# A kernel of two transformer stages with expert look-up: fourteen more load buffers for the first up units, spreading from unit 64, and five row slots

## The chip, the cores and the metric

The kernel runs on one core of one Trainium2 chip. Its time is the device time of one execution in microseconds; the median of several runs is compared. Engines are named as in the profile: PE is TensorE, DVE the vector engine, ACT the scalar engine, POOL the pool engine (GpSimd), SP the queue engine that issues loads.

## What is computed

A block with attention and a state-space mixer is followed by a second block, whose last part is the place of the change: for 256 tokens h a look-up in 16,384 experts. A query picks 16 experts for each of eight heads, u and v are tables of 16,384 rows of 1,024 numbers, and

```python
def chunk(ht):
    t = ht.shape[0]
    q = (ht @ wq).reshape(t, PEER_HEADS, 2, PEER_DK)
    sa = jnp.einsum('thd,hnd->thn', q[:, :, 0], keys[0]).astype(jnp.float32)
    sb = jnp.einsum('thd,hnd->thn', q[:, :, 1], keys[1]).astype(jnp.float32)
    ...
    eidx = jnp.take_along_axis(cidx, pos, axis=-1)
    g = jax.nn.softmax(top, axis=-1).astype(ht.dtype)
    u = u_tab[eidx]
    v = v_tab[eidx]
    a = jax.nn.gelu(jnp.einsum('thkd,td->thk', u, ht))
    return jnp.einsum('thk,thkd->td', g * a, v)
```

## The kernel before, in words

The tokens of the look-up are treated in two ways. For the first ND = 176 tokens the kernel multiplies with the whole tables: 128 "up units" of u and 128 "down units" of v, each 128 experts wide and 512 KB, are loaded one after the other. For the other 80 tokens it gathers the picked rows: 80 "row passes" with rows of u and 80 with rows of v, each pass one indirect load of 128 rows of 4 KB and one DVE instruction over 128x1024.

In order of time the last part has these stages. The query projection (16 units `peer_wq`). The early up units 0 to N_EARLY - 1 = 49 on PE, while DVE picks the experts (`pick`), first for the second half of the tokens, whose row numbers are known early, then for the first. ACT writes the gelu of two units at once into X (`u_early`). Then the late up units 50 to 127. Beside them the gates are spread: for each of ND/4 = 44 steps s (four tokens each) DVE, POOL and ACT write one-hot rows of the picked experts (`one_hot`), PE multiplies them into a bank ("spread", four small matmuls), and DVE and ACT multiply the bank into X (`empty_gates`, `copy_rest`). Late units are multiplied with their gates by `u_late`. At last the down stage: each of 256 chunks (two per down unit) is cut into a high part by ACT and a low part by DVE, and PE multiplies it with X.

Row passes run on DVE in the order of the list `passes`: N_FIRST = 16 inside the second pick, then those up to N_BETWEEN = 23 before the spread steps, those up to N_LATE = 94 within them, and the remaining 66 within the down stage, evenly over 250 chunk steps (`pass_step`).

What sets the order is written out by hand. The generator `spread_steps` yields, for every half unit, which one-hot, spread, emptying and row pass stand there, and PE, DVE, ACT and POOL each run through the same sequence and pick their own; every engine carries out its instructions in that order and waits for semaphores. One-hot s needs the buffer of spread s - 2. Gather n (`gather`, on POOL) needs the slot of pass n - 4.

Loads of weights are issued by SP in the order of `plan`, into a ring of NRAW = 4 buffers: up unit n + 4 is loaded when unit n is done, a down unit when the one four before it has been cut. In the trace of the kernel before, L609 is SP's load, L615 PE's matmul, L2093 a row pass of u, L1342 a row pass of v, L3125 a gather, L3136 a one-hot on POOL, L1336 and L1339 DVE's tensor_tensor and tensor_scalar (one-hots among them), L2232 and L2229 ACT's copies and activations.

## Time and profile before

| what | us |
|---|---|
| median of 3 runs | 1458.18 |
| lowest, highest | 1457.92, 1467.05 |
| the profiled execution | 1462.89 |
| its span, first to last instruction | 1461.1 |
| PE busy | 1400.8 (96%) |
| DVE busy | 1143.9 (78%) |
| POOL busy | 392.2 (27%) |
| DMA, mean over the span | 249 GB/s |

A windows row gives, for a stretch, each engine's busy time with the number of its instructions, then the granted share of PE's clock, the busy share of the 16 DMA engines and what they moved. A timeline row gives start, duration, instruction, and in brackets the idle time before it with what ended it. In the profile a matmul of two fp32 operands stands as two records; the count of an up unit is so 16. Times in rows count from the start of the span.

### The profile page before, as it was taken

The numbers are of one execution on the slowest core, as the hardware profiler recorded it, in microseconds if no ns is written. First come the engines' busy times: TensorE is split into PE (matmuls) and PEld (weight loads), VectorE is DVE, ScalarE is ACT, GpSimd is POOL, SyncE is SP. The second block draws the span as 40 slices with busy tenths as digits, with TensorE's granted clock in tenths as the row PEclk, the third lists the DMA queues.
The fourth block names the chain that finished last, engine by engine and source line by source line (L and its number), as shares of the span: only waits on it lengthen the run. The fifth ranks groups of instructions, "written<-read, shape, count | busy, mean of one in ns | idle before, by whom it ended". The sixth has DMA issues, their size and how long they took to land.

```text
span 1461.1 us, 28173 instructions
## 1 busy us (share of the span) xinstructions
PE 1400.8 (96%) x10866; PEld 1301.5 (89%) x10866; DVE 1143.9 (78%) x2296; ACT 773.2 (53%) x1576; POOL 392.2 (27%) x421
## 2 busy tenths in 40 slices
PE   7999999998999999999889999999999999999998
PEld 6668998877879988888789999899999999999998
DVE  4676996787668889866657899676777699899987
ACT  5785886753355555566454200344443466666655
POOL 7620001000300000001100022589887343333430
PEclk9999999999999999999999999999999999999999
DMA  7305554651369899652344699989999899999995
GB/s 241 101 30 169 179 170 151 192 180 40 138 219 345 310 323 344 244 172 88 111 127 143 186 334 334 373 313 363 356 351 363 310 363 352 359 353 349 358 340 177
DMA packets 100003, 363.47 MB, mean 249 GB/s; under 512 B 11152, under 2 KB 11152, under 8 KB 99744
## 3 DMA queue, kind: packets, MB, share of 16 engines
q1 hardware_dynamic: 67536, 244.45, 48.5%
q0 software_dynamic: 24560, 89.95, 17.0%
q10 hardware_dynamic: 7776, 27.27, 5.1%
q8 instruction: 89, 1.46, 0.4%
q14 instruction: 42, 0.34, 0.1%
HBM read 360.58 MB, written 1.05 MB: 248 GB/s over the span
## 4 chain that ended last, share of the span: by engine, by line
PE 74%; DVE 9%; DMA 9%; ACT 4%; issue 3%; POOL 0%; DVEq 0%; ACTq 0%; SPq 0%
PE ps L615 72%; DMA arena<-in_peer_v 5%; DVE w_lo L1336 3%; DVE arena L1336 2%; ACT w_hi L2232 2%; DVE arena L1342 2%; ACT arena L2229 1%; DMA arena<-in_u_rows,arena 1%; DMA arena<-in_peer_u 1%; PE ps L821 1%; DMA arena<-in_w_ff 1%; PE ps L948 0%; DVE act_hi_lo L1336 0%; PE ps L778 0%; DVE arena L2093 0%
## 5 line engine op out<-in xcount | busy, mean ns | idle before, releaser
L1336 DVE TENSOR_TENSOR w_lo<-arena,w_hi 128x512 fp32r<-128x512 f32 x680 | 455.4, 689 | 166.5 <-ACT w_hi L2232 162.3
L2232 ACT ACTIVATE w_hi<-arena 128x512 fp32r<-128x512 f32 x680 | 417.6, 625 | 294.3 <-PE ps L615 219.8
L615 PE MATMUL ps<-act_hi_lo,w_hi 128*128 128x256 f32 (+1 forms) x2496 | 554.8, 315 | 12.4 <-DVE w_lo L1336 5.2
L615 PE MATMUL ps<-arena 128*128 128x176 f32 (+9 forms) x4858 | 480.7, 280 | 23.5 <-DVE arena L1339 7.5
L615 PEld LDWEIGHTS ps<-arena 128*128 128x128 f32 (+3 forms) x4858 | 455.2, 166 | 44.9 <-issue 17.4
L615 PE MATMUL ps<-act_hi_lo,w_lo 128*128 128x176 f32 (+1 forms) x1760 | 455.7, 259 | 0.1
L615 PEld LDWEIGHTS ps<-act_hi_lo,w_hi 128*128 128x128 f32 x2496 | 421.6, 190 | 21.3 <-ACT w_hi L2232 9.1
L615 PEld LDWEIGHTS ps<-act_hi_lo,w_lo 128*128 128x128 f32 x1760 | 336.4, 191 | 0.1
L615 PE MATMUL ps<-w_hi,act_hi_lo 128*128 128x512 f32 (+2 forms) x960 | 304.5, 392 | 11.5 <-DVE w_lo L1336 5.0
L1336 DVE TENSOR_TENSOR arena<-arena 128x512 f32<-128x512 f32 (+17 forms) x298 | 183.7, 625 | 63.2 <-ACT arena L2229 56.9
L615 PEld LDWEIGHTS ps<-w_hi,act_hi_lo 128*128 128x128 f32 x960 | 181.0, 190 | 55.3 <-issue 13.7
L615 PE MATMUL ps<-w_lo,act_hi_lo 128*128 128x512 f32 (+2 forms) x480 | 185.9, 387 | 0.0
L3125 POOL DMA_INDIRECT arena<-in_v_rows,arena x80 | 123.7, 1546 | 192.4 <-DVE arena L1342 179.9
L2229 ACT ACTIVATE arena<-ps 128x512 f32<-128x512 f32 (+19 forms) x138 | 55.3, 429 | 188.8 <-PE ps L615 172.5
L3125 POOL DMA_INDIRECT arena<-in_u_rows,arena x80 | 95.0, 1187 | 204.3 <-DVE arena L1946 128.9
L2229 ACT ACTIVATE arena<-arena 128x128 f32<-128x128 f32 (+8 forms) x256 | 122.2, 491 | 49.2 <-DVE arena L1336 19.6
L2961 POOL TENSOR_TENSOR arena<-arena 128x32 f32<-128x32 f32 (+1 forms) x130 | 55.5, 441 | 317.1 <-ACT arena L2232 271.2
L2232 ACT ACTIVATE arena<-ps 128x512 f32<-128x512 f32 (+21 forms) x160 | 70.2, 454 | 108.4 <-DVE arena L1336 71.8
L2093 DVE SCALAR_TENSOR_TENSOR arena<-arena 128x1024 f32<-128x1024 f32 x80 | 97.6, 1228 | 17.3 <-DMA arena<-in_u_rows,arena 15.9
L1342 DVE SCALAR_TENSOR_TENSOR arena<-arena 128x1024 f32<-128x1024 f32 (+5 forms) x100 | 107.1, 1071 | 1.5 <-DMA arena<-in_v_rows,arena 0.9
L615 PEld LDWEIGHTS ps<-w_lo,act_hi_lo 128*128 128x128 f32 x480 | 91.2, 190 | 16.6
L3136 POOL TENSOR_SCALAR arena<-arena 128x128 f32<-128x128 f32 x66 | 88.9, 1350 | 4.9 <-DVE arena L2021 1.5
(105 smaller groups left out, 681.3 us busy)
## 6 DMA issues: line engine op xcount, KB each, us to landing
arena<-in_w_ff SPq DMA_DIRECT2D x128, 512.0 KB
arena<-in_peer_u SPq DMA_DIRECT2D x128, 512.0 KB
arena<-in_peer_v SPq DMA_DIRECT2D x128, 512.0 KB
arena<-in_w_ada ACTq DMA_DIRECT2D x48, 512.0 KB, 5.5
arena<-in_w_glu SPq DMA_DIRECT2D x16, 512.0 KB
arena<-in_peer_wq SPq DMA_DIRECT2D x16, 512.0 KB
arena<-in_w_in SPq DMA_DIRECT2D x12, 512.0 KB
arena<-in_w_conv SPq DMA_DIRECT2D x12, 512.0 KB
```

The source lines that it names most:

```text
L615: return e.matmul(o, l, r, start=start, stop=stop)
L821: ins = e.transpose(pb(bk, 2 * nk, 128)[:, h * nk + kb, :], att.s(u)[:, h, kb * 128:(kb + 1) * 128], ident)
L1336: return e.tensor_tensor(o, a, b, op)
L1342: return e.scalar_tensor_tensor(out=o, in0=a, scalar=s, in1=b, op0=op0, op1=op1)
L2093: ins = e.scalar_tensor_tensor(out=slot, in0=slot, scalar=1.0, in1=row_h[g], op0=ALU.mult, op1=ALU.mult, accum_out=a)
L2229: return e.activation(o, a, f, **k)
L2232: return e.activation(o, a, ACT.Copy)
L2961: return e.tensor_tensor(o, a, b, op)
L3125: e.indirect_dma_start(row_slot(n), None, T[f"{kind}_rows"], bass.IndirectOffsetOnAxis(ap=row_at[:, p:p + 1].bitcast(U32), axis=0)).then_i ...
L3136: ins = e.tensor_scalar(ob[:, k, :], iota, ibT[:, n:n + 1], gT[:, n:n + 1], ALU.is_equal, ALU.mult)
```

## The change

Fourteen buffers join the ring for the up units: ten in the place of the mixed activations (the low end of the arena, where X will be written), four at 16384. They serve units up to the one whose result is written there (`last_u`), the last of them up to unit 63. Up units 0 to 11 are loaded among the query loads: eight after query load 3, one each after 5, 7, 9 and 11 (`U_AHEAD`). From unit 12 on a load goes into the buffer that has been in use longest of those that may still serve it. N_EARLY goes from 50 to 64, N_BETWEEN from 23 to 36 (20 passes between the second pick and the spread steps, where there were 7), N_LATE from 94 to 104. Row slots go from four to five, so that gather n needs the slot of pass n - 5. The gelu of the first 32 rows' products is done ahead of the spread steps, and the copy of the tokens to hU is used from unit N_EARLY + 2.

```diff
--- before.py
+++ after.py
@@
 EPS = 1e-6
 UNIT = 1024
 NRAW = 4
+N_LOW, N_MORE = 10, 14
+U_AHEAD = {3: range(8), 5: (8,), 7: (9,), 9: (10,), 11: (11,)}
 CUT = 512
 NHL = 4
+N_SLOTS = 5
 AHEAD = 3
-N_EARLY = 50
+N_EARLY = 64
 ND = 176
 
 OFF_X = 0
...
@@
     len_of = {name: sum(plan[i][0] == name for i, _ in chunks) for name in end}
     first_u = next(i for i, x in enumerate(plan) if x[0] == "peer_u")
 
+    buffers = [ar[:, OFF_RING + UNIT * n:OFF_RING + UNIT * n + UNIT] for n in range(NRAW)]
+    buffers += [ar[:, UNIT * n:UNIT * n + UNIT] for n in range(N_LOW)]
+    buffers += [ar[:, 16384 + UNIT * n:16384 + UNIT * n + UNIT] for n in range(4)]
+    free_after = ["ring"] * NRAW + ["mixed"] * N_LOW + ["window"] * 2 + ["keys"] * 2
+    last_u = [127] * NRAW + [min(N_EARLY - 1, 2 * (UNIT * n // (2 * ND)) + 1) for n in range(N_LOW)]
+    last_u += [N_EARLY - 1] * 4
+    first_order = list(range(NRAW, NRAW + N_LOW + 2)) + [None] * NRAW + list(range(NRAW + N_LOW + 2, NRAW + N_MORE))
+
+    buffer_of, used_before, load_of = [], [], []
+    used = {}
+    for i in range(len(plan)):
+        u = i - first_u
+        b = i % NRAW
+        if 0 <= u < len(first_order):
+            b = b if first_order[u] is None else first_order[u]
+        elif 0 <= u < 128:
+            b = min((x for x in used if last_u[x] >= u), key=lambda x: used[x][0])
+        buffer_of.append(b)
+        used_before.append(used[b][0] if b in used else None)
+        load_of.append(used[b][1] + 1 if b in used else 1)
+        used[b] = i, load_of[i]
+
     def raw(i):
-        o = OFF_RING + (i % NRAW) * UNIT
-        return ar[:, o:o + plan[i][2]]
+        return buffers[buffer_of[i]][:, 0:plan[i][2]]
 
     def raw_in(i):
-        return ring_in[i % NRAW], 16 * (i // NRAW + 1)
+        return ring_in[buffer_of[i]], 16 * load_of[i]
+
+    def load_order():
+        first_q = first_u - 16
+        early = [u for us in U_AHEAD.values() for u in us]
+        for i in range(len(plan)):
+            if i - first_u not in early:
+                yield i
+            for u in U_AHEAD.get(i - first_q, ()):
+                yield first_u + u
 
     def raw_piece(n):
         i, c = chunks[n]
@@
 
     passes = [("u", p) for p in range(N_ROWS)] + [("v", p) for p in range(N_ROWS)]
     nth = {x: n for n, x in enumerate(passes)}
-    N_PASS, N_FIRST, N_BETWEEN, N_LATE, N_ONES = len(passes), 16, 23, 94, 3
-    U_COPY = N_EARLY + 4
+    N_PASS, N_FIRST, N_BETWEEN, N_LATE, N_ONES = len(passes), 16, 36, 104, 3
+    U_COPY = N_EARLY + 2
 
     def row_group(p):
         return sum(p >= f for f in ROW_FIRST[1:3])
@@
     row_bank = (6, 7, 2, 3, 4, 5)
 
     def row_slot(g):
-        return V(QP + 1024 * (g % 4), 1024)
+        return V((QP, QP + 1024, QP + 2048, QP + 3072, OFF_GB + 1024)[g % N_SLOTS], 1024)
 
     def pass_step(n):
 
@@
     def sync_program(e):
         e.dma_start(V(OFF_SM, SMN), T["small"]).then_inc(small_in, 16)
         e.wait_ge(x_in[0], 16)
-        for i, (_, source, _, _) in enumerate(plan):
-            before = i - NRAW
+        for i in load_order():
+            source, before, free = plan[i][1], used_before[i], free_after[buffer_of[i]]
             if i == 1:
                 e.wait_ge(x_in[1], 16)
-            if before >= 0 and plan[before][0] == "peer_u":
+            if before is not None and plan[before][0] == "peer_u":
                 e.wait_ge(*u_done["unit", before - first_u])
-            elif before >= 0:
+            elif before is not None:
                 e.wait_ge(lo_cut.sem, last_cut[before] + 1)
-            e.dma_start(raw(i), source).then_inc(ring_in[i % NRAW], 16)
+            elif free == "mixed":
+                for c in (0, 2, 4, 6):
+                    e.wait_ge(*alo_cut["mixed1", c])
+            elif free == "window":
+                e.wait_ge(*masked["window", window_att.n - 1])
+            elif free == "keys":
+                e.wait_ge(*mm_done["key_scores", 0, 3])
+            e.dma_start(raw(i), source).then_inc(ring_in[buffer_of[i]], 16)
 
     def tensor_program(e):
         at = dict(n=0)
@@
                 e.wait_ge(*bent["rows", g])
                 tt(products, products, row_g[:, own], ALU.mult).then_inc(*rows_v("gated", g))
                 e.wait_ge(*rows_v["gated", g])
-            e.wait_ge(gather_in[n % 4], 16 * (n // 4 + 1))
+            e.wait_ge(gather_in[n % N_SLOTS], 16 * (n // N_SLOTS + 1))
             if kind == "u":
                 ins = e.scalar_tensor_tensor(out=slot, in0=slot, scalar=1.0, in1=row_h[g], op0=ALU.mult,
                                              op1=ALU.mult, accum_out=a)
@@
                 e.wait_ge(*gated["spread", ND // 4 - 1])
             elif j == 1:
                 e.wait_ge(*gated["u", 63])
+        for n in sorted(after_products):
+            if n < N_BETWEEN:
+                row_gelu(after_products[n])
         for what, *a in spread_steps():
             if what == "units":
                 copy_rest(waiting)
@@
         def gather(n):
 
             kind, p = passes[n]
-            if n >= 4:
-                e.wait_ge(*rows_v["pass", n - 4])
+            if n >= N_SLOTS:
+                e.wait_ge(*rows_v["pass", n - N_SLOTS])
             e.indirect_dma_start(row_slot(n), None, T[f"{kind}_rows"],
                                  bass.IndirectOffsetOnAxis(ap=row_at[:, p:p + 1].bitcast(U32), axis=0)
-                                 ).then_inc(gather_in[n % 4], 16)
+                                 ).then_inc(gather_in[n % N_SLOTS], 16)
 
         def one_hot(s):
             oa, ob = one_hots(s)
@@
             ins.then_inc(*ones_p("b", s))
 
         e.wait_ge(*pick_v["rows"])
-        for n in range(N_FIRST + 4):
+        for n in range(N_FIRST + N_SLOTS):
             gather(n)
         e.wait_ge(*bank[6]["picked", 0])
         one_hot(0)
-        for n in range(N_FIRST + 4, N_BETWEEN + 3):
-            if n == N_FIRST + 6:
+        for n in range(N_FIRST + N_SLOTS, N_BETWEEN + N_SLOTS - 1):
+            if n == N_FIRST + N_SLOTS + 2:
                 one_hot(1)
-            if n == N_BETWEEN + 2:
+            if n == N_BETWEEN + N_SLOTS - 2:
                 one_hot(2)
             gather(n)
         for what, *a in spread_steps():
             if what == "ones" and a[0] >= N_ONES:
                 one_hot(*a)
             elif what == "row":
-                gather(a[0] + 3)
-        for n in range(N_LATE + 3, N_PASS):
+                gather(a[0] + N_SLOTS - 1)
+        for n in range(N_LATE + N_SLOTS - 1, N_PASS):
             gather(n)
 
     programs = ((nc.tensor, tensor_program), (nc.vector, vector_program), (nc.scalar, scalar_program),
```

On SP the query and up loads now alternate (in the rows, `in_peer_wq` is the query projection's weights and `in_peer_u` the up units'). SP's place around the query projection, before:

```order
L609 DMA arena<-in_w_conv 128x1024 x12
L609 DMA arena<-in_w_out 128x1024 x8
L609 DMA arena<-in_peer_wq 128x1024 x16
L609 DMA arena<-in_peer_u 128x1024 x128
L609 DMA arena<-in_peer_v 128x1024 x128
```

and now:

```order
L649 DMA arena<-in_w_out 128x1024 x8
L649 DMA arena<-in_peer_wq 128x1024 x4
L649 DMA arena<-in_peer_u 128x1024 x8
L649 DMA arena<-in_peer_wq 128x1024 x2
L649 DMA arena<-in_peer_u 128x1024
L649 DMA arena<-in_peer_wq 128x1024 x2
L649 DMA arena<-in_peer_u 128x1024
L649 DMA arena<-in_peer_wq 128x1024 x2
L649 DMA arena<-in_peer_u 128x1024
L649 DMA arena<-in_peer_wq 128x1024 x2
```

Twelve up loads stand ahead of the last query loads, the other 116 behind them.

On POOL, from the first gather on (`in_u_rows` is a gather, L3136 and L3179 are one-hots, one for even steps and two for odd ones), before:

```order
L3125 DMA arena<-in_u_rows,arena 128x1024 x20
L3136 TENSOR_SCALAR arena<-arena 128x128
L3125 DMA arena<-in_u_rows,arena 128x1024 x2
L3136 TENSOR_SCALAR arena<-arena 128x128 x2
L3125 DMA arena<-in_u_rows,arena 128x1024 x3
L3136 TENSOR_SCALAR arena<-arena 128x128
L3125 DMA arena<-in_u_rows,arena 128x1024 x6
L3136 TENSOR_SCALAR arena<-arena 128x128 x2
L3125 DMA arena<-in_u_rows,arena 128x1024
L3136 TENSOR_SCALAR arena<-arena 128x128
L3125 DMA arena<-in_u_rows,arena 128x1024 x2
L3136 TENSOR_SCALAR arena<-arena 128x128 x2
```

and now:

```order
L3168 DMA arena<-in_u_rows,arena 128x1024 x21
L3179 TENSOR_SCALAR arena<-arena 128x128
L3168 DMA arena<-in_u_rows,arena 128x1024 x2
L3179 TENSOR_SCALAR arena<-arena 128x128 x2
L3168 DMA arena<-in_u_rows,arena 128x1024 x16
L3179 TENSOR_SCALAR arena<-arena 128x128
L3168 DMA arena<-in_u_rows,arena 128x1024 x5
L3179 TENSOR_SCALAR arena<-arena 128x128 x2
L3168 DMA arena<-in_u_rows,arena 128x1024 x2
L3179 TENSOR_SCALAR arena<-arena 128x128
L3168 DMA arena<-in_u_rows,arena 128x1024
L3179 TENSOR_SCALAR arena<-arena 128x128 x2
```

Sixteen gathers instead of three stand between one-hots 1 and 2, five instead of six between one-hots 2 and 3; after that the pattern of one or two gathers to a one-hot step goes on.

On DVE, from the seventeenth row pass on (L2093 and L2133; the pair L1336 and L1339, L1376 and L1379 over 128x512 and 128x128 is a one-hot, the form `ps,arena` an emptying), before:

```order
L2093 SCALAR_TENSOR_TENSOR arena<-arena 128x1024 x6
L1336 TENSOR_TENSOR arena<-arena 128x512
L1339 TENSOR_SCALAR arena<-arena 128x128
L2093 SCALAR_TENSOR_TENSOR arena<-arena 128x1024 x4
L1336 TENSOR_TENSOR arena<-ps,arena 128x54x4
L2093 SCALAR_TENSOR_TENSOR arena<-arena 128x1024
L1336 TENSOR_TENSOR arena<-arena 128x2x4
L2093 SCALAR_TENSOR_TENSOR arena<-arena 128x1024
L1336 TENSOR_TENSOR arena<-arena 128x512
L1339 TENSOR_SCALAR arena<-arena 128x128
```

and now:

```order
L2133 SCALAR_TENSOR_TENSOR arena<-arena 128x1024 x19
L1376 TENSOR_TENSOR arena<-arena 128x512
L1379 TENSOR_SCALAR arena<-arena 128x128
L2133 SCALAR_TENSOR_TENSOR arena<-arena 128x1024 x3
L1376 TENSOR_TENSOR arena<-ps,arena 128x66x4
L2133 SCALAR_TENSOR_TENSOR arena<-arena 128x1024
L1376 TENSOR_TENSOR arena<-arena 128x2x4
L2133 SCALAR_TENSOR_TENSOR arena<-arena 128x1024
L1376 TENSOR_TENSOR arena<-arena 128x512
L1379 TENSOR_SCALAR arena<-arena 128x128
```

Nineteen passes instead of six stand ahead of one-hot 2, and five instead of six between one-hots 2 and 3.

## Rows read from the trace of the kernel before

**Rows 1.** The page: busy time, share of the span, instructions of each engine.

```profile
PE 1400.8 (96%) x10866; PEld 1301.5 (89%) x10866; DVE 1143.9 (78%) x2296; ACT 773.2 (53%) x1576; POOL 392.2 (27%) x421
```

**Rows 2.** Busy time by stage; the first row names the columns.

```profile
core 0: us, PE busy (x) PEld busy (x) DVE busy (x) ACT busy (x) POOL busy (x), PEclk, DMA share, GB/s
716.00:797.00 81.00, 75.49 (x558) 70.72 (x558) 52.53 (x164) 39.90 (x76) 1.12 (x2) 1.00 0.43 133
...
847.00:921.00 74.00, 72.77 (x486) 71.93 (x485) 72.47 (x253) 9.84 (x18) 23.25 (x21) 1.00 0.95 349
...
953.00:1145.00 192.00, 191.78 (x1357) 191.81 (x1358) 141.93 (x270) 76.85 (x226) 162.38 (x128) 0.99 0.96 352
...
1158.00:1440.00 282.00, 275.26 (x2005) 271.51 (x2005) 257.37 (x377) 174.41 (x310) 100.72 (x62) 1.00 0.95 347
```

**Rows 3.** Busy time by ten microseconds, same columns.

```profile
940.00:950.00 10.00, 6.69 (x46) 6.18 (x44) 5.67 (x11) 1.62 (x5) 5.24 (x5) 0.98 1.03 410
950.00:960.00 10.00, 6.78 (x38) 6.81 (x39) 6.82 (x16) 4.55 (x13) 9.32 (x6) 0.67 0.54 187
```

**Rows 4.** Timeline of PE: start, duration, instruction, idle before it, releaser.

```profile
859.87 1.31 PE L615 MATMUL ps<-arena 128*128 128x176 f32 x7 [0.78 <-DMA arena<-in_peer_u]
...
953.22 1.19 PE L615 MATMUL ps<-arena 128*128 128x128 f32 x4 [5.79 <-DVE arena L1339]
...
1158.78 0.40 PE L615 MATMUL ps<-act_hi_lo,w_hi 128*128 128x352 f32 x1
...
1452.94 1.03 PE L1242 MATMUL ps<-arena 128*128 128x128 f32 x8
```

**Rows 5.** Timeline of ACT, the evacuation of units 48 and 49.

```profile
923.52 0.46 ACT L2229 ACTIVATE arena<-ps 128x352 f32<-128x352 f32 x1 [4.52 <-PE ps L615]
```

**Rows 6.** Timeline of SP, the loads that it issued.

```profile
728.43 11.65 SPq L609 DMA_DIRECT2D arena<-in_peer_wq  x2
...
872.48 45.67 SPq L609 DMA_DIRECT2D arena<-in_peer_u  x20
...
930.68 3.61 SPq L609 DMA_DIRECT2D arena<-in_peer_u  x2
```

**Rows 7.** Timeline of POOL and DVE at the first spreads.

```profile
937.28 0.96 POOL L3125 DMA_INDIRECT arena<-in_u_rows,arena  x1 [1.18 <-DVE arena L2093]
...
943.45 1.22 DVE L2093 SCALAR_TENSOR_TENSOR arena<-arena 128x1024 f32<-128x1024 f32 x1 [1.32 <-issue]
...
945.86 1.23 DVE L2093 SCALAR_TENSOR_TENSOR arena<-arena 128x1024 f32<-128x1024 f32 x1 [0.89 <-DMA arena<-in_u_rows,arena]
...
952.54 0.34 DVE L1339 TENSOR_SCALAR arena<-arena 128x128 f32<-128x128 f32 x1
```

**Rows 8.** Groups of POOL's instructions, 954.2 to 1031.4, then 953 to 1150.

```profile
L3136 POOL TENSOR_SCALAR arena<-arena 128x128 f32<-128x128 f32 x24 | 37.8, 1581 | 0.6
L3125 POOL DMA_INDIRECT arena<-in_u_rows,arena x27 | 32.4, 1202 | 7.4 <-issue 5.0 <-DVE arena L2093 2.4
...
L3136 POOL TENSOR_SCALAR arena<-arena 128x128 f32<-128x128 f32 x61 | 81.4, 1338 | 2.9 <-PE ps L615 1.4
L3125 POOL DMA_INDIRECT arena<-in_u_rows,arena x49 | 60.8, 1241 | 15.5 <-issue 8.8 <-DVE arena L2093 6.7
L3125 POOL DMA_INDIRECT arena<-in_v_rows,arena x18 | 23.0, 1276 | 11.2 <-DVE arena L1342 5.1 <-issue 2.4 <-DVE arena L1336 1.9
```

**Rows 9.** Timeline of POOL, two pairs of one-hots; a windows row of the second.

```profile
1006.30 1.58 POOL L3136 TENSOR_SCALAR arena<-arena 128x128 f32<-128x128 f32 x2
...
1025.53 4.69 POOL L3136 TENSOR_SCALAR arena<-arena 128x128 f32<-128x128 f32 x2
...
1025.50:1030.20 4.70, 4.70 (x36) 4.70 (x35) 4.70 (x11) 2.31 (x6) 4.67 (x2) 1.00 0.97 361
```

**Rows 10.** The chain of waits: one stretch of PE's work.

```profile
1253.42 26.96 PE ps L615 x200
```

**Rows 11.** Who waited for whom, 1158 to 1440: total us, times, longest.

```profile
ACT w_hi L2232 <- DMA arena<-in_peer_v: 59.4, 58, 2.9
```

More of the change, by code:

```diff
@@ L143, in signal @@
         return signals[-1]
-    ring_in = [sem(f"ring_in{i}") for i in range(NRAW)]
+    ring_in = [sem(f"ring_in{i}") for i in range(NRAW + N_MORE)]
     x_in = [sem(f"x_in{t}") for t in range(2)]
@@ L150, in build_in @@
     ssm_in, win_in, out_done = sem("ssm_in"), sem("window_bias_in"), sem("out_done")
-    gather_in = [sem(f"gather_in{i}") for i in range(4)]
+    gather_in = [sem(f"gather_in{i}") for i in range(N_SLOTS)]
     ada_in = [sem(f"ada_in{i}") for i in range(4)]
```

## The prediction

> **What bounds the kernel now.** I read the page first: TensorE is busy 96% of the span and the pool engine 27% [rows 1]. So a gain can only be time in which TensorE stands still or runs slowly, and I went to the windows view for the stages that the change touches [rows 2]. There the reader should compare TensorE's busy time with the length, and the DMA share with 1. The query projection (716 to 797) moves 133 GB/s at a share of 0.43: there is room for more loads. In the pick stage (847 to 921) the vector engine is the full one, 72.5 of 74 us. From 953 to 1145 TensorE never stops (191.8 of 192), the pool engine works 162 us of it although its mean over the span is low, and the DMA engines are at 0.96. In the last stage they are at 0.95 and TensorE loses 7 of 282 us visibly.
>
> Then the timeline of PE shows the single stalls [rows 4]: 0.78 us for an up unit's load, and 5.79 us before the fourth spread, at 947 to 953. After that one the granted clock is 0.67 for ten microseconds [rows 3], between the 1.2 and the 2.4 GHz level. The releaser of the long stall is the second half of DVE's one-hot, which ends at 952.88 [rows 7]; ahead of it on DVE stand row passes, 2.41 us apart where one costs 1.23, because a gather issued at 937.28 is used at 945.86, 8.6 us later, with four slots [rows 7].
>
> **Own pace of each stage.** SP issues 20 unit loads with (45.67 - 0.33)/19 = 2.39 us between them, and 3.28 us where a spread lies between [rows 6]: a unit costs TensorE 2.39 us, a spread 0.89. Unit 49 ends at 923.5 [rows 5], the last up unit at 1158.8 [rows 4]: 235.3 us. 78 units and 44 spreads need 186.4 + 39.2 = 225.6, so 9.7 us are lost. The down stage runs from 1158.8 to 1452.9 [rows 4]: 294.2 us. It has 2,048 matmuls and 48 small ones for the row sums; 200 in 26.96 us [rows 10] make 0.135 us each, 282.5 us together. 11.7 us are lost; the DMA of the down units is what the scalar engine's cut waits for, 58 times and 59.4 us [rows 11].
>
> **The change part by part.**
>
> *Fourteen more buffers, loads ahead.* Twelve loads, 6.3 MB, go into the query projection. Eight follow query load 3, which is issued at 728.4; the next query load comes at 739.8 [rows 6]. At the 410 GB/s that ten other microseconds reach [rows 3] the eight take 10.2 us, so the next query load is hardly held, and it belongs to the fifth of the sixteen query units, which TensorE reaches some 13 us into the projection: cost nothing. If that cover failed, TensorE would wait for a query load of some 1.3 us; I keep 0 to 2. SP waits for the mixed activations before the burst, which the query projection needs anyway. In return the unit load that was late at 859 is early: -0.8 [rows 4].
>
> *Spreading from unit 64.* The first fourteen of the 78 units now run before any spread. Unit 63 ends at 923.5 - 0.8 + 14 x 2.39 = 956.1. From there 64 units and 44 spreads need 153.0 + 39.2 = 192.2: 1148.3 without any wait. That is 10.5 us before the 1158.8 of today, the 0.8 included: what all of the stalls are worth.
>
> *Twenty passes in between, five slots.* DVE has from 921 until unit 63 for passes 16 to 34, then its one-hot 2 waits for spread 0 (962 or so). With five slots and the same latency the distance is (8.6 + 1.6)/5 = 2.0 us instead of 2.4 to 2.6; the first five passes find their rows landed. That makes pass 34 end near 927 + 14 x 2.0 = 955 to 958, in time. Behind the pool engine's one-hot 2, which waits for the same spread, stand five gathers and then one-hot 3: about 963 + 1 + 8.6 us for the row of pass 39, then one-hot 3 on DVE at 974 to 975, just when spread 3 is due. I take 1.5 us of the 5.8 as left; the bounds are 0 and 7 (the old stall with its slow clock). The gelu of the first 32 rows now stands on ACT ahead of the spread steps and waits for pass 31, some 950: hidden behind unit 63.
>
> *Denser spreading.* The same 41 one-hot steps and 67 gathers now have to go beside 64 units, not 78. TensorE's distance between spreads falls from 144/44 x 1.19 + 0.89 = 4.8 us (144 half units) to 116/44 x 1.19 + 0.89 = 4.03 us. The pool engine makes 1.5 one-hots and 1.6 gathers a spread. From 954.2 to 1031.4 it made 24 and 27 with 2.4 us of waits for others [rows 8]: (77.2 - 2.4)/16 = 4.67 us a spread. From 953 to its last piece of the stage at 1145.5, 61 and 67 with 15.1 us of waits [rows 8]: 177.4/40.7 = 4.36. The new mix has 0.1 gathers fewer a spread (68/44 against 1.65) at about 1.5 us: 4.21 and, from the first stretch, 4.46. Both are above 4.03. So **the pool engine takes TensorE's place** as what sets the spreads: 41 x (4.21 - 4.03) = 7 us; bounds 0 (it keeps up) and 41 x 0.43 = 18. I take 7, nearest to the row over the whole stage.
>
> Why it is so slow shows in its timeline: two one-hots take 1.58 us alone and 4.69 where DVE is busy nearly throughout [rows 9]. The Trainium skill, "SBUF — State Buffer", section "SBUF: two separate sides", speaks against this change here: it says that the two engines share a port pair as an exclusive lock, so that the loser fully blocks while an instruction with two SBUF inputs runs. By that rule a spread would cost the pool engine its own 1.5 x 0.79 + 1.55 x 1.2 = 3.0 us and DVE's passes and one-hot, 1.55 x 1.22 + 1.0 = 2.9, on top: an estimated 5.9 us, and a kernel of some 1520. The trace agrees only in part: today's 4.8 us with nobody waiting is less than that.
>
> *DMA in the late units.* 64 unit loads (four of them down units) and 67 gathers in 192 us are 358 GB/s, against 352 from 953 to 1145 [rows 2] and 410 at best [rows 3]: enough, and the wait of about 1 us before the last units stays (0 to 4). Up stage in sum: 1148.3 + 1.5 + 7 + 1 = 1157.8, 1.0 us earlier than now.
>
> *Ten passes fewer in the down stage.* 347 GB/s over 282 us [rows 2] are 186 transfers of 0.524 MB; ten fewer ask for 328 GB/s. DVE loses ten passes of 1.2 us, from 257 to 245 us [rows 2, 7]. A ring that waited at 95% load should wait much less at 90%: I take 7.5 of the 11.7 us back, bounds 0 and 11.7.
>
> Sum: -1.0 - 7.5 = -8.5 us. The profiled execution took 1462.9 us, so it would take 1454.4; it lies 4.7 us above the median of 1458.2, and against that median the forecast is **1450**. A change of 14.6 us (1%) is what a few runs can tell.
>
> **The rivals.** (A) The pool engine keeps up: it shares its port only while DVE works, and from 1050 on it had room. Then the 7 us are gained too: 1443, and 1438 with the whole of the down stage's waits. For it: nobody waited for it in this trace, and what the whole stretch makes less than its first part shows that it can be quicker. Against: [rows 8]. (B) Slower: the pool engine stays at the 4.8 us a spread of today, since DVE's work on the same port is packed denser. 41 x 0.79 = 32 us against 15.5 gained elsewhere: 1475. It cancels the gain at 4.03 + 15.5/41 = 4.41 and is slower by over 1% from 4.76 on; the worst stretch measured was 4.67. (It is a milder form of the lock that the Trainium skill's page on SBUF describes.) (C) The down stage waits as before, since its four buffers, not the bandwidth, set the latency that it can bear: 1457. (D) The early loads bring nothing, because SP's queue stands at a wait in order (for the key scores before units 16 and 17, then for units not yet done): the lead is gone before the gathers start and the units wait again: 1458.
>
> **How the numbers follow.** Forecast 0.41, A 0.27, B 0.08, C 0.17, D 0.07. The range 1438 to 1461 holds A to D without B and the upper bounds. Faster by over 1% (under 1443.6): most of A and a seventh of the forecast, 0.28. Slower by over 1% (over 1472.8): B's upper half and mishaps, 0.06. Within: 0.66.
>
> **What would show it.** Query projection near 210 GB/s and as long as now; no wait for up loads until 1140; unit 63 done at 956 and a PE stall at spread 3 under 2 us. Between 975 and 1140 PE waits for the pool engine's one-hots, with 4.2 us between spreads and the pool engine busy over 90%; if instead spreads stand 4.03 apart and PE is busy throughout, A holds. In the down stage ACT's waits for down units fall from 59 to under 35 us and the stage from 294 to 287. It is wrong if the up stage ends before 1150 or after 1166.

## The result: 1.2% slower, and the profile after

The changed kernel took **1475.5 us** (median of 4 runs, 1471.9 to 1479.0), the kernel before 1458.1 (4 runs, 1456.8 to 1467.1): a ratio of 1.0117, 95% interval 1.0086 to 1.0149. The forecast was 1450 in a range of 1438 to 1461. The number is rival B's, by chance: B had spreads 4.8 us apart and the gain in the down stage, and the runs show 4.48 and no gain.

The profiled execution of the changed kernel took 1475.04 us, 12.1 more than the profiled one of before (1462.9). The page gives the busy times and the chain that ended last:

```profile
PE 1400.4 (95%) x10866; PEld 1296.4 (88%) x10866; DVE 1144.9 (78%) x2290; ACT 769.8 (52%) x1570; POOL 382.5 (26%) x421
...
PE 59%; DVE 14%; DMA 11%; POOL 7%; ACT 4%; issue 4%; ACTq 0%; DVEq 0%; SPq 0%
```

The chain of the kernel before reads:

```profile
PE 74%; DVE 9%; DMA 9%; ACT 4%; issue 3%; POOL 0%; DVEq 0%; ACTq 0%; SPq 0%
```

The page's first row reads like [rows 1]: no engine's busy time has grown by more than 1.0 us, and TensorE's is equal to 0.4 us. What is new is POOL's 7% in the chain, where it had 0%. The windows view places it (columns as in [rows 2]: length, busy us of each engine with its instructions, granted clock, DMA share, GB/s):

```profile
709.00:790.00 81.00, 76.41 (x558) 72.16 (x557) 52.73 (x164) 39.77 (x76) 1.12 (x2) 0.98 0.61 210
840.00:914.00 74.00, 72.19 (x485) 71.92 (x485) 72.47 (x254) 9.83 (x18) 24.19 (x22) 1.00 0.89 322
971.00:1150.00 179.00, 162.82 (x1144) 158.57 (x1144) 138.21 (x249) 71.92 (x212) 164.16 (x122) 1.00 0.94 337
1166.00:1448.00 282.00, 272.00 (x1969) 266.93 (x1969) 242.41 (x362) 170.56 (x305) 74.32 (x51) 1.00 0.90 322
```

Read the third row against its like in [rows 2]: TensorE was busy 191.8 of 192 us and is busy 162.8 of 179, while POOL works 164.2, 92%. In the last row the DMA share has fallen from 0.95 to 0.90, as forecast, but TensorE's busy time in a window of 282 us has fallen too, from 275.3 to 272.0. The early loads stand where they were meant to, in SP's timeline:

```profile
716.60 5.29 SPq L649 DMA_DIRECT2D arena<-in_peer_wq  x2
722.08 5.45 SPq L649 DMA_DIRECT2D arena<-in_peer_u  x8
732.88 3.33 SPq L649 DMA_DIRECT2D arena<-in_peer_wq  x2
```

**A common clock for all kernels.** The part ahead of the query projection, which no kernel here changes, ended between 704.9 and 716.1 us in the profiles. So the table counts from each profile's first query load. "Spread 3" and "spread 43" are the starts of the fourth and the last spread, "pitch" is the mean distance between them, and "one-hot" and "gather" are the mean durations on POOL in between. The last column is the down stage, first matmul to last.

| profiled kernel | spread 3 | spread 43 | down start | pitch | POOL busy | one-hot | gather | down stage |
|---|---|---|---|---|---|---|---|---|
| before | 237.1 | 427.3 | 442.7 | 4.75 | 85% | 1.32 | 1.26 | 294.3 |
| after | 261.7 | 440.9 | 457.0 | 4.48 | 92% | 1.37 | 1.33 | 299.1 |
| e1 | 260.8 | 421.3 | 437.0 | 4.01 | 83% | 1.17 | 1.39 | 297.4 |
| e2 | 239.0 | 436.5 | 453.5 | 4.94 | 86% | 1.33 | 1.24 | 303.2 |
| e3 | 234.1 | 424.3 | 438.3 | 4.75 | 83% | 1.15 | 1.36 | 298.6 |
| e4 | 260.9 | 426.6 | 442.9 | 4.14 | 92% | 1.52 | 1.16 | 301.0 |
| e5 | 236.9 | 427.3 | 442.3 | 4.76 | 85% | 1.24 | 1.33 | 283.5 |
| e6 | 260.4 | 420.1 | 436.5 | 3.99 | 83% | 1.15 | 1.39 | 283.5 |
| e7 | 238.3 | 429.8 | 444.2 | 4.79 | 85% | 1.26 | 1.34 | 284.3 |
| e8 | 236.8 | 427.1 | 441.1 | 4.76 | 86% | 1.26 | 1.33 | 289.2 |
| e9 | 239.8 | 432.6 | 448.6 | 4.82 | 81% | 1.56 | 1.29 | 294.8 |
| e10 | 235.7 | 426.9 | 442.9 | 4.78 | 70% | 1.31 | 1.24 | 297.4 |
| e11 | 264.8 | 444.6 | 460.7 | 4.50 | 89% | 1.28 | 1.34 | 298.9 |
| e12 | 261.3 | 437.8 | 453.5 | 4.41 | 91% | 1.30 | 1.32 | 283.6 |
| e13 | 260.0 | 418.7 | 434.6 | 3.97 | 80% | 1.46 | 1.31 | 283.5 |
| e14 | 260.0 | 419.8 | 434.4 | 3.99 | 77% | 1.02 | 1.00 | 298.9 |

By this clock the change costs 457.0 - 442.7 = 14.3 us up to the down stage and 4.8 in it, 19.1 together; the medians say 17.5. One profile is one execution: the profiled one of e4 took 1465.6 us, the longest of its 11, where the median is 1456.9.

**POOL as the new bound.** The timelines of POOL, then of PE, at two spreads of the changed kernel:

```profile
1042.83 2.00 POOL L3168 DMA_INDIRECT arena<-in_u_rows,arena  x1 [0.16 <-issue]
1044.87 1.66 POOL L3179 TENSOR_SCALAR arena<-arena 128x128 f32<-128x128 f32 x1
1046.70 2.01 POOL L3168 DMA_INDIRECT arena<-in_u_rows,arena  x1 [0.17 <-issue]
1049.02 0.94 POOL L3168 DMA_INDIRECT arena<-in_u_rows,arena  x1 [0.30 <-issue]
1049.99 2.81 POOL L3179 TENSOR_SCALAR arena<-arena 128x128 f32<-128x128 f32 x2
1052.97 2.04 POOL L3168 DMA_INDIRECT arena<-in_u_rows,arena  x1 [0.16 <-issue]
```

```profile
1046.63 4.71 PE L655 MATMUL ps<-arena 128*128 128x128 f32 x32 [0.35 <-DVE arena L1379]
1052.90 3.37 PE L655 MATMUL ps<-arena 128*128 128x128 f32 x23 [1.56 <-issue]
```

POOL's one-hots end at 1046.53 and at 1052.80, and each time the spread starts 0.10 us later; 20 of the 41 spreads from the fourth on start 0.10 us after a one-hot of POOL, two more within 0.17. Ahead of 16 of those 20 TensorE stood still, and these 16 waits, 16.3 us together, are all that it waited between spread 3 and the last. PE's row names DVE's one-hot, or "issue", yet DVE's one had ended 0.38 and 4.15 us earlier. Where a wait is put down to an engine that had long been done, look at the engine beside it.

What makes POOL slow shows when DVE's row passes of the same microseconds are laid beside its rows:

```profile
1046.63 1.21 DVE L2133 SCALAR_TENSOR_TENSOR arena<-arena 128x1024 f32<-128x1024 f32 x1
...
1052.92 1.23 DVE L2133 SCALAR_TENSOR_TENSOR arena<-arena 128x1024 f32<-128x1024 f32 x1 [0.69 <-DMA arena<-in_u_rows,arena]
```

POOL's gathers at 1046.70 and 1052.97 began just after a pass had begun, and they ended 0.87 and 0.86 us after it; the gather at 1049.02 met no pass and took 0.94. It is so throughout: of the 62 gathers between spreads 3 and 43, the 25 that began inside a pass all ended 0.82 to 0.88 us after the end of that pass, 1.73 us long in the mean, and the other 37 took 1.05. A one-hot takes 0.79 us alone; the 23 of 60 that began inside a pass took 1.80 in the mean, and each ended 0.65 us or more after the pass. So POOL's instruction stands until the running pass is over. The passes themselves are hardly longer: 1.27 us in the mean where an instruction of POOL ran when they began, 1.24 where none did.

### The profile page after: what moved, and what is told of

Read it like the earlier page. It is cut to its first block, busy times and chain, and to the rows that moved or that the text cites. A ratio compares the mean times of both kernels' runs of the same rounds, so it can differ in the third digit from the quotient of the medians.

```text
span 1473.2 us, 28181 instructions
## 1 busy us (share of the span) xinstructions
PE 1400.4 (95%) x10866; PEld 1296.4 (88%) x10866; DVE 1144.9 (78%) x2290; ACT 769.8 (52%) x1570; POOL 382.5 (26%) x421
## 3 DMA queue, kind: packets, MB, share of 16 engines
q8 instruction: 89, 1.46, 0.4%
HBM read 360.58 MB, written 1.05 MB: 245 GB/s over the span
## 4 chain that ended last, share of the span: by engine, by line
PE 59%; DVE 14%; DMA 11%; POOL 7%; ACT 4%; issue 4%; ACTq 0%; DVEq 0%; SPq 0%
PE ps L655 58%; DMA arena<-in_peer_v 7%; DVE w_lo L1376 3%; POOL arena L3168 3%; POOL arena L3179 3%; DVE arena L1376 3%; DVE arena L1382 2%; ACT w_hi L2272 2%; DMA arena<-in_u_rows,arena 2%; ACT arena L2269 1%; DVE arena L2133 1%; DMA arena<-in_v_rows,arena 1%; PE ps L861 1%; DMA arena<-in_w_in 1%; DVE act_hi_lo L1376 1%
## 5 line engine op out<-in xcount | busy, mean ns | idle before, releaser
L1376 DVE TENSOR_TENSOR w_lo<-arena,w_hi 128x512 fp32r<-128x512 f32 x680 | 455.8, 689 | 178.5 <-ACT w_hi L2272 174.4
L655 PEld LDWEIGHTS ps<-w_hi,act_hi_lo 128*128 128x128 f32 x960 | 180.0, 189 | 55.9 <-issue 13.5
L1376 DVE TENSOR_TENSOR arena<-arena 128x512 f32<-128x512 f32 (+15 forms) x292 | 181.4, 629 | 43.4 <-ACT arena L2269 36.2
L3168 POOL DMA_INDIRECT arena<-in_v_rows,arena x80 | 112.5, 1406 | 209.0 <-DVE arena L1382 192.7
L2269 ACT ACTIVATE arena<-arena 128x128 f32<-128x128 f32 (+7 forms) x256 | 122.1, 492 | 65.1 <-DVE arena L1376 21.0
L2133 DVE SCALAR_TENSOR_TENSOR arena<-arena 128x1024 f32<-128x1024 f32 x80 | 98.1, 1233 | 38.0 <-DMA arena<-in_u_rows,arena 37.8
L1382 DVE SCALAR_TENSOR_TENSOR arena<-arena 128x1024 f32<-128x1024 f32 (+5 forms) x100 | 107.4, 1074 | 2.0 <-DMA arena<-in_v_rows,arena 1.2
L655 PEld LDWEIGHTS ps<-w_lo,act_hi_lo 128*128 128x128 f32 x480 | 90.8, 189 | 16.3
L3179 POOL TENSOR_SCALAR arena<-arena 128x128 f32<-128x128 f32 x66 | 90.0, 1367 | 6.1 <-PE ps L655 2.9
```

The source lines that it names most:

```text
L655: return e.matmul(o, l, r, start=start, stop=stop)
L1376: return e.tensor_tensor(o, a, b, op)
L1382: return e.scalar_tensor_tensor(out=o, in0=a, scalar=s, in1=b, op0=op0, op1=op1)
L2133: ins = e.scalar_tensor_tensor(out=slot, in0=slot, scalar=1.0, in1=row_h[g], op0=ALU.mult, op1=ALU.mult, accum_out=a)
L2269: return e.activation(o, a, f, **k)
L3168: e.indirect_dma_start(row_slot(n), None, T[f"{kind}_rows"], bass.IndirectOffsetOnAxis(ap=row_at[:, p:p + 1].bitcast(U32), axis=0)).then_i ...
```

## The experiments

Each median stands beside that of the kernel before in runs of the same chip: 1461.4 for e1 to e4, 1460.6 for e5 to e8, 1459.1 for e9 to e12, 1459.4 for e13 and e14.

**e1: POOL makes one half one-hot a spread instead of one and a half; the scalar engine takes the others.** An edit of the changed kernel.

```diff
-        return "pool" if k == 1 or k == 2 and s % 2 else "scalar"
+        return "pool" if k == 1 else "scalar"
```

> The change with one line different: the pool engine's second one-hot of every odd step is made by ACT, so that the pool engine makes 1 one-hot a spread instead of 1.5 (gathers as before). Theory P (the pool engine's own work sets the distance of the spreads, 4.48 us in the changed kernel): the distance falls by about half a one-hot, 0.5 x 1.5 = 0.75 us, down to TensorE's own 4.03; 41 x 0.45 = 18 us less, so 1457 to 1460. Rival Q (DVE's queue or late rows set it, and the pool engine is only the last in the line): the distance stays at 4.3 to 4.5 and the time at 1468 to 1476. If ACT becomes the next one that is waited for, PE waits for ACT in the late stage and the distance is 4.2 to 4.3.

1452.5 us (1449.1 to 1460.5, 10 runs), ratio 0.9953 (0.9931 to 0.9975): 23 us less than the changed kernel, and 4.5 less than the lower end of what was expected. The pitch falls from 4.48 to 4.01, TensorE's own. POOL's work was the bound.

**e2: ten more row passes ahead of the down stage, in the kernel before.**

```diff
-    N_PASS, N_FIRST, N_BETWEEN, N_LATE, N_ONES = len(passes), 16, 23, 94, 3
+    N_PASS, N_FIRST, N_BETWEEN, N_LATE, N_ONES = len(passes), 16, 23, 104, 3
```

> The kernel before with N_LATE 104 instead of 94 and nothing else: ten row passes more within the spread steps, ten fewer in the down stage. Theory W (the down stage waits by bandwidth, as I predicted): down stage 294 to 287 us; the pool engine needs 4.36 + 0.23 x 1.5 = 4.7 us a spread, still under the 4.87 of the kernel before, so the time is about 1451. Theory L (the four buffers and the latency of a load set the waits, ten gathers fewer do nothing): down stage 293 to 295, time 1457 to 1459. If the up stage cannot carry ten passes more, it grows by up to 6 us and the time is 1460 or more.

1476.2 us (1471.1 to 1481.6, 4 runs), ratio 1.0124 (1.0078 to 1.0171). This one number costs as much as the whole change: 10.8 us up to the down stage, more than was expected under any theory, and no gain in it (303.2). Most of the standing still is at the two ends of the spreads: TensorE stood 7.9 us ahead of spread 3 (5.8 in the kernel before) and 4.1 ahead of the last, each time until 0.10 us after POOL's one-hot, and 1.3 between.

**e3: the early loads alone.** The changed kernel with the spreading as before.

```diff
-N_SLOTS = 5
+N_SLOTS = 4
-N_EARLY = 64
+N_EARLY = 50
-    N_PASS, N_FIRST, N_BETWEEN, N_LATE, N_ONES = len(passes), 16, 36, 104, 3
-    U_COPY = N_EARLY + 2
+    N_PASS, N_FIRST, N_BETWEEN, N_LATE, N_ONES = len(passes), 16, 23, 94, 3
+    U_COPY = N_EARLY + 4
```

> The change's buffers and early loads alone: N_EARLY 50, N_BETWEEN 23, N_LATE 94, four row slots, copy used from unit 54, as in the kernel before. Theory (the loads ahead are hidden and free): the wait of 0.8 us at an up unit's load goes, everything else as before: 1456 to 1458. Rival (they hold up the query projection, or the lead makes the unit loads crowd the gathers out, so that the passes before the spreads are later): 1460 to 1466, with the stall before the fourth spread over 6 us.

1459.4 us (1454.3 to 1466.3, 10 runs), ratio 0.9996 (0.9974 to 1.0019). The loads neither cost nor bring anything that can be measured.

**e4: the changed kernel with 94 passes ahead of the down stage.** The counterpart of e2.

```diff
-    N_PASS, N_FIRST, N_BETWEEN, N_LATE, N_ONES = len(passes), 16, 36, 104, 3
+    N_PASS, N_FIRST, N_BETWEEN, N_LATE, N_ONES = len(passes), 16, 36, 94, 3
```

> The change with N_LATE 94 instead of 104: ten passes and gathers move from the spread steps to the down stage, where 66 stand again. Theory P: 58 passes instead of 68 over 44 spreads are 0.23 gathers a spread fewer, about 1.5 us each for the pool engine: distance 4.48 to 4.15, up stage 13 us shorter. The down stage with theory L unchanged: 1462; with theory W 7 us longer: 1469. Rival Q (not the pool engine): distance unchanged, 1475 or more.

1456.9 us (1454.5 to 1465.6, 11 runs), ratio 0.9979 (0.9961 to 0.9998): 18.6 us less than the changed kernel. Eight gathers fewer between spreads 3 and 43 (54 for 62) bring the pitch to 4.14, with POOL still 92% busy. (4.48 - 4.14) x 40 / 8 = 1.7 us for each, more than the 1.33 that its own issue takes.

**e5: a fifth load buffer for the down units, in the kernel before.** It lies in a part of the memory that is free by then.

```diff
+    buffers = [OFF_RING + UNIT * n for n in range(NRAW)] + [23552]
...
+        if plan[i][0] == "peer_v":
+            b = min(range(NRAW + 1), key=lambda x: used.get(x, (-1, 0))[0])
```

> The kernel before with a fifth load buffer for the down units alone (at 23552, unused then). Theory L (a buffer is in use for the 6.4 us until its load is cut and the 2.7 us of cutting, 9.1 us a round of four units, which is over the 8.7 us that TensorE needs for them): with five buffers the loop allows 1.83 us a unit, TensorE's 2.17 becomes the bound again, the down stage falls from 294 to 283 to 287 and the time by 7 to 11 us. Theory W (bandwidth: the DMA engines are at 0.95): the latency grows with the fifth load in flight, the down stage stays at 291 to 295 and the time within 3 us of before.

1446.8 us (1446.2 to 1447.7, 4 runs), ratio 0.9905 (0.9887 to 0.9923). The down stage takes 283.5 us, within 1 us of the 282.5 that its matmuls need. Its windows row:

```profile
1156.00:1438.00 282.00, 281.92 (x2089) 281.80 (x2087) 267.60 (x391) 188.25 (x329) 84.80 (x62) 1.00 0.94 347
```

TensorE is busy 281.9 of 282 us at a DMA share of 0.94 and 347 GB/s, the very load at which four buffers lost 11.7 us [rows 2]. So neither the DMA engines' load nor DVE's 268 us bound this stage.

**e6: e1 with the fifth down buffer**, the two edits shown above, in the changed kernel.

> The change with the pool engine's second one-hot given to ACT (as in e1) and with the fifth buffer for the down units. Theory L: both gains add, e1's 1452.5 less 10 to 14: 1439 to 1443. Theory W: as e1, 1450 to 1453.

1439.4 us (1434.0 to 1443.3, 4 runs), ratio 0.9853 (0.9819 to 0.9886). It beats both kernels. Its windows of the spreads and of the down stage show TensorE at work throughout:

```profile
971.40:1131.00 159.60, 158.83 (x1144) 158.61 (x1145) 136.09 (x251) 90.29 (x257) 133.04 (x103) 1.00 0.99 377
1148.00:1430.00 282.00, 281.92 (x2088) 281.85 (x2088) 257.45 (x380) 187.25 (x327) 59.25 (x51) 1.00 0.90 326
```

**e7 and e8: the down stage of the kernel before without its gathers, and with its passes over 8 columns.**

```diff
-            e.wait_ge(gather_in[n % 4], 16 * (n // 4 + 1))
+            if n < N_LATE + 3:
+                e.wait_ge(gather_in[n % 4], 16 * (n // 4 + 1))
...
-        for n in range(N_LATE + 3, N_PASS):
-            gather(n)
```

```diff
+                w = 8 if n >= N_LATE else 1024
-                ins = stt(row_acc[g], slot, a, row_acc[g], ALU.mult, ALU.add)
+                ins = stt(row_acc[g][:, 0:w], slot[:, 0:w], a, row_acc[g][:, 0:w], ALU.mult, ALU.add)
```

> The kernel before without the 63 gathers of rows in the down stage; DVE still makes its 66 passes, over old rows. It leaves out part of the v sum of the 80 tokens. Theory L with the loads' latency made longer by the gathers beside them: the latency falls from 6.4 to about 5, the loop to 7.8 us, under TensorE's 8.7: down stage 283 to 285, time -9 to -11. If the gathers are hidden (the latency is the loads' own, or DVE's passes are what holds the buffers): down stage 291 to 295.

> The kernel before with the gathers kept, but DVE's passes in the down stage over 8 columns instead of 1024 (it leaves out part of the v sum of the 80 tokens). Theory L: DVE's 1.28 us per pass no longer stand between ACT's cut and DVE's, the hold falls by 0.3 to 0.5 us of 9.1: down stage 284 to 289. If DVE's place in the loop is nothing: 292 to 295. If both e7 and e8 shorten the stage fully, the loop is only just too long, and small things decide it.

e7: 1448.1 us (4 runs), ratio 0.9918 (0.9896 to 0.9941), down stage 284.3. e8: 1449.3 us (4 runs), 0.9925 (0.9902 to 0.9949), down stage 289.2. Either alone takes 12.5 and 11.3 us away by the medians, as can be where a loop of four buffers is only a little too long. The loop, averaged over units 4 to 127 of the down stage: from the issue of a load to the scalar engine's cut of it 6.40 us in the kernel before and 6.51 after; from there to the end of DVE's second low cut, which frees the buffer, 2.70 and 2.73. That makes 9.10 and 9.24 us for four units, where TensorE needs 34.7/16 x 4 = 8.68 (sixteen units take it 34.7 us in e5). SP issues the next load 0.03 us after the release, so nothing else is in the turn, and 32 rounds with some 3 us at the start are the 294 and 299 us measured; this sum only says that the ring is closed, and the proof that it bounds the stage is e5. Without the passes the hold is 2.19 us. The chain of waits of the changed kernel shows one turn:

```profile
1205.87 7.11 DMA arena<-in_peer_v
1212.98 0.02 issue
1213.00 0.64 ACT w_hi L2272
1213.64 0.03 issue
1213.67 0.04 DVE w_lo L1376
1213.70 0.57 issue
1214.28 1.28 DVE arena L1382
1215.56 0.61 DVE w_lo L1376
1216.17 0.14 issue
1216.30 5.64 PE ps L655 x40
```

A load takes 7.1 us, and a row pass of 1.28 us (L1382) stands on DVE between the two low cuts of a unit that came late.

**e9 and e10: e1's edit in e2 and in the kernel before.**

> The kernel before with ten more row passes in the up stage (104 instead of 94; that alone gave 1476) and with all of the pool engine's half one-hots given to the scalar engine (one a spread instead of one and a half). Theory P (the pool engine's work sets the spreads): the pitch falls from 4.94 to about 4.75 and the time by 41 x 0.2 = 8 us, more if the stall ahead of spread 3 shrinks too: 1464 to 1470. Rival Q (what costs is the latency of the gathered rows over four slots, which ten more rows stretch): the pitch stays at 4.9 and the time within 4 us of 1476.

> The kernel before with the pool engine's second half one-hots given to the scalar engine and nothing else changed. Theory P: in the kernel before TensorE itself sets the spreads (own pace 4.8, measured 4.75), so the pool engine's relief brings nothing: pitch 4.75, time within 4 us of 1460. Rival R (the pool engine holds this kernel up as well, hidden in the stall ahead of spread 3 and in the end of the up stage): 5 us or more faster, 1455 or less.

e9: 1463.0 us (1459.4 to 1468.0, 10 runs), ratio 1.0033 (1.0008 to 1.0057), 13 us less than e2, pitch 4.82 for 4.94. e10: 1458.3 us (10 runs), 0.9994 (0.9970 to 1.0018). So POOL's relief brings nothing where the spreads stand 4.75 us apart and TensorE sets them, and it takes back part of e2's cost where ten more gathers are to be made.

**e11: the changed kernel with four row slots.**

```diff
-N_SLOTS = 5
+N_SLOTS = 4
```

> The changed kernel with four row slots instead of five. Theory P: spreading is set by the pool engine, not by the rows' latency, so the pitch stays at 4.48; the stall ahead of spread 3 comes back in part: 1476 to 1481. Rival S (the fifth slot does harm, since more gathers in flight slow the loads and lengthen the issue of each): under 1470, pitch 4.3 or less. Rival Q (rows' latency is near to binding): pitch over 4.7 and 1485 or more.

1480.8 us (1475.7 to 1485.5, 4 runs), ratio 1.0171 (1.0122 to 1.0221). The pitch stays (4.50), and spread 3 comes 3.1 us later, so by the profile the fifth slot helps at the start of spreading (the intervals of the two ratios overlap). It is no part of the loss.

**e12: the changed kernel with the fifth down buffer alone.** e6 without e1's edit.

> The changed kernel with a fifth load buffer for the down units alone. Theory L (the loop of four buffers, 6.5 + 2.7 us, is longer than TensorE's 8.69 for four units): the down stage falls from 299.1 to 283.5 as in the kernel before with five, the up stage stays with its pitch of 4.48: 1475.5 - 15.5 = 1460, so what is left against the kernel before with five (1447) is the up stage alone, 13 us. Rival (the down stage is held by something that ten fewer passes brought): it stays above 290 and the time above 1467.

1456.3 us (1454.4 to 1462.2, 10 runs), ratio 1.0001 (0.9977 to 1.0024). The down stage is 283.6 us; what stands against e5 (1446.8) is the up stage.

**e13: e6 with 94 passes ahead of the down stage.**

> The changed kernel with the pool engine's half one-hots on the scalar engine, the fifth down buffer, and 94 instead of 104 row passes before the down stage. With the pool engine relieved, the pitch is TensorE's own 4.0 with 104 passes already, and with five buffers the down stage stands at TensorE's own 283.5 with 56 or 66 passes. So theory: no difference from the same kernel with 104 (1439): 1437 to 1442. Rival: the ten passes still cost through the DMA share of 0.99 in the up stage, 3 us or more faster: under 1436; or the down stage with 66 gathers and five buffers loses again: over 1443.

1438.1 us (1436.6 to 1439.7, 4 runs), ratio 0.9857 (0.9798 to 0.9916), no different from e6. Once POOL is relieved and the ring has five buffers, it doesn't matter on which side the ten passes stand.

**e14: the changed kernel with DVE's up-stage row passes over 8 columns, all loads and gathers kept.**

```diff
+            w = 8 if N_BETWEEN <= n < N_LATE else 1024
-                ins = e.scalar_tensor_tensor(out=slot, in0=slot, scalar=1.0, in1=row_h[g], op0=ALU.mult,
+                ins = e.scalar_tensor_tensor(out=slot[:, 0:w], in0=slot[:, 0:w], scalar=1.0, in1=row_h[g][:, 0:w], op0=ALU.mult,
```

> The changed kernel with the vector engine's 68 row passes of the up stage (passes 36 to 103) over 8 columns instead of 1024; it leaves out most of the rows' products and part of their sum. All gathers and all loads stay. Theory V (the vector engine's passes beside it stretch the pool engine's instructions): the pool engine's one-hot falls from 1.37 us to 1.0 or less, the pitch from 4.48 to TensorE's own 4.0 and the time by some 19 us: 1456. Rival T (the pool engine's time is its own, or set by the DMA work in flight): one-hots of 1.3 us, pitch 4.4, time 1470 or more.

1452.8 us (1447.7 to 1463.4, 10 runs), ratio 0.9968 (0.9936 to 1.0000). Groups of POOL's instructions between spreads 3 and 43, with busy us and mean ns behind the bar and the idle time ahead of them last; first the changed kernel:

```profile
L3179 POOL TENSOR_SCALAR arena<-arena 128x128 f32<-128x128 f32 x60 | 82.1, 1371 | 1.6
L3168 POOL DMA_INDIRECT arena<-in_u_rows,arena x36 | 46.9, 1303 | 7.8 <-issue 7.2 <-DVE arena L2133 0.6
L3168 POOL DMA_INDIRECT arena<-in_v_rows,arena x26 | 35.2, 1356 | 5.6 <-issue 4.7 <-DVE arena L1382 0.6 <-DVE arena L2133 0.3
```

and e14:

```profile
L3180 POOL TENSOR_SCALAR arena<-arena 128x128 f32<-128x128 f32 x60 | 61.0, 1020 | 16.4 <-PE ps L655 15.4
L3169 POOL DMA_INDIRECT arena<-in_u_rows,arena x36 | 36.0, 999 | 10.3 <-issue 5.7 <-DVE arena L2134 4.6
L3169 POOL DMA_INDIRECT arena<-in_v_rows,arena x28 | 28.1, 1005 | 10.2 <-DVE arena L1382 5.7 <-issue 4.4
```

POOL's instructions between these spreads, two gathers more among them, take 125.1 us instead of 164.2, and POOL now waits 15.4 us for TensorE. The windows row of e14 shows what did not do it:

```profile
970.60:1131.00 160.40, 159.54 (x1150) 159.28 (x1150) 75.39 (x253) 73.58 (x215) 123.91 (x123) 1.00 1.00 383
```

The DMA engines carry more than in the changed kernel (share 1.00, 383 GB/s, against 0.94 and 337), and the gathers are issued faster. What went is DVE's work, from 138 to 75 us.

## Why the prediction was wrong

**Right in mechanism and size.** Unit 63 ended 240.6 us after the first query load; 956.1 - 716.1 = 240.0 was forecast. The early loads were free (e3). The stall ahead of spread 3 was 1.53 us, forecast 1.5. The own pace of spreads, 4.03 us, was measured as 3.97 to 4.01 where POOL was relieved.

**Right in mechanism, wrong in size: "Denser spreading ... 41 x (4.21 - 4.03) = 7 us".** POOL did take TensorE's place. But the pitch was 4.48, and spreads 3 to 43 took 179.2 us against 159.8 in e14: 19.4 us. The step took the mean over the whole stage of before, since it was "nearest to the row over the whole stage", with a one-hot at 1.34 us and a gather at 1.25. The changed kernel had 1.37 and 1.32, plus 0.38 us idle between instructions: 1.5 x 1.37 + 1.55 x 1.32 + 0.38 = 4.48. The upper bound, from the first and dense stretch, was 4.46. That was the row to take: the change packs DVE's work denser, and e14 shows that this work is what stretches POOL's. That 4.46 meets 4.48 so closely is in part chance, since its terms were 1.58 and 1.20. The ten passes moved ahead of the down stage are most of it: with them the changed kernel has 14.1 us more up to the down stage than without (457.0 and 442.9 in e4), and they alone cost 10.8 in the kernel before (e2), though there mostly at the two ends.

The old trace held a warning that was read past. The prediction ends the stall of 5.79 us with DVE's one-hot at 952.88, as PE's row says, and counts for rival A that "nobody waited for it in this trace". But POOL's row is

```profile
948.35 4.77 POOL L3136 TENSOR_SCALAR arena<-arena 128x128 f32<-128x128 f32 x2
```

It ends at 953.12, and the spread began at 953.22 [rows 4], 0.10 us later as in the changed kernel. TensorE was waiting for POOL already, though DVE's one-hot had come only 0.24 us before.

Of the lock on the port pair, which the Trainium skill describes ("SBUF — State Buffer", section "SBUF: two separate sides"), the estimate was 5.9 us a spread. The trace agrees that POOL, as the loser, is blocked until the pass is over: 25 gathers of 25 ended 0.82 to 0.88 us behind it. What was wrong is the sum, which laid the whole of DVE's passes and one-hots on top of POOL's work. An instruction of POOL loses only the rest of a pass that is running when it begins, and 37 of the 62 gathers began in none. So DVE's full passes added (164.2 - 125.1)/40 = 1.0 us to POOL's work a spread, about half of their own 1.55 x 1.22 = 1.9, and the pitch was 4.48. Weighed as a direction, the rule would have moved the choice to the upper bound.

**Wrong: "A ring that waited at 95% load should wait much less at 90%: I take 7.5 of the 11.7 us back".** The load fell to 0.90 and none of the 7.5 us came back. Profiles with 66 passes in a four-buffer down stage took 294.3, 297.4, 298.6 and 301.0 us, those with 56 took 294.8, 297.4, 298.9, 298.9, 299.1 and 303.2: means of 297.8 and 298.7. Rival C (0.17) named the mechanism, and e5, e6, e12 and e13 show it: with a fifth buffer the stage takes 283.5 us at either count and at a share of 0.94 or 0.90. Of the 12 us between the forecast 286.7 and the measured 299.1, 7.5 are the gain that did not come; the other 5 lie within the scatter of the profiles with 66 passes. The profile had said so: the scalar engine waited 58 times for a load that had been issued only when its buffer came free [rows 11]. That is a loop's length, not a rate.

The two errors are 19.4 - 7 = 12 and 299.1 - 286.7 = 12 us, 24 together; the medians differ by 25.5 from the forecast. By the common clock the up stage ended 457.0 - (1157.8 - 716.1) = 15.3 us late: 12 by the first, and 3 that no run here assigns.

**Open.** Whether ten gathers and passes fewer bring a little with four buffers was not settled. Without any gathers the stage took 284.3 us (e7), 13.5 less than the mean of 297.8, so ten of the 66 would be worth 2 us by proportion, an estimate; the scatter hides so much, but not 7.5. And e9's down stage of 294.8 against e2's 303.2, with the same work in it, shows that a ring a little too short scatters by some 8 us by itself, so of e9's 13 us against e2 the common clock gives only 4.9 to the up stage.

**What the change is worth.** With both bounds lifted, the changed kernel takes 1439.4 and 1438.1 us (e6, e13) and the kernel before 1446.8 (e5); since e1's edit brings the kernel before nothing (e10), the change itself is then worth 7 to 9 us. The kernel before with both edits was not run. Of the 10.5 us that all stalls were said to cost, most was there to be had.

## What to carry to other kernels

A ring of buffers is checked by its loop: issue to use, plus use to release, against the number of buffers times the consumer's pace. If the loop is longer, a lighter DMA load need not help, while one more buffer can give everything back (14 us here for 512 KB). When a change packs the same work into less time, the price of a helper engine's instruction is to be read in the densest stretch of the old trace, not as a mean over the stage; and an engine with 27% over the span can still be the next bound of one stage. Before a trace is said to hold no wait for an engine, the ends of all engines that feed the waiting one are compared.

## What the runs showed of the hardware that was not expected

- POOL's instructions stretch with DVE's work beside them: a one-hot of 128x128 took 1.37 us with full row passes and 1.02 with short ones, the issue of a gather 1.32 and 1.00, single ones 2.0 beside a row pass. So the issue of an indirect transfer is held up like arithmetic: begun inside a row pass, it ends 0.82 to 0.88 us after the pass, and begun outside one it takes 0.94 to 1.0 us in most cases.
- 383 GB/s at a DMA share of 1.00 did not slow TensorE in e14 (159.5 of 160.4 us busy), nor did 377 in e6.
- With five buffers a down load took 8.2 us from issue to its cut instead of 6.5, because it waited for its turn, and no time was lost: it landed 6.70 us after its issue in e12 (five buffers) and 6.02 in e11 (four).
